# Hybrid encoder trunk on one core: the first feed-forward down projection multiplies 256 tokens at a time instead of 512

## The chip, the cores and the metric

The kernel runs on one core of one Trainium2 chip. The metric is the device time of one execution in microseconds (us), from the first to the last instruction of the program. The trace comes from one profiled execution on that core.

## The reference

Two layers, 512 frames (tokens) of 1024 features, everything in float32. Each layer does this:

```
x = x + 0.5 * swiglu(rmsnorm(x, ffn1_norm), ffn1_w_gate, ffn1_w_up, ffn1_w_down)
h = rmsnorm(x, mix_norm); proj = h @ w_in
x = x + concat(ssd_mixer(...), hgrn2_mixer(...)) @ w_out
x = x + 0.5 * swiglu(rmsnorm(x, ffn2_norm), ffn2_w_gate, ffn2_w_up, ffn2_w_down)

def swiglu(h, w_gate, w_up, w_down):
    return (jax.nn.silu(h @ w_gate) * (h @ w_up)) @ w_down
```

A last rmsnorm follows the second layer. The hidden width of a feed-forward part is 2816. The part of interest is the last product of swiglu in the first feed-forward part, `(512 x 2816) @ (2816 x 1024)`, once per layer.

## The kernel before, in words

Activations lie with features on the partitions and the 512 tokens along the free dimension, so x is 8 tiles of 128 x 512 and the hidden activations are 22 tiles of 128 x 512. Weights are cut into 128 x 128 pieces. A float32 product is made of three products of a reduced format (fp32r): each operand is split into a high part and a low part, and high·high, high·low and low·high are added up in one PSUM bank. `products` (L1463 to L1469) issues these three matmuls for one 128 x 128 weight piece against all 512 tokens: L1467 is weight high with activation high, L1468 weight high with activation low, L1469 weight low with activation high. The hardware loads the stationary weights anew for each of them, which the trace shows as one LDWEIGHTS (engine PEld) for each MATMUL (engine PE).

A feed-forward part has two stages. The up stage makes gate and up for 22 hidden tiles (44 weight blocks of 8 pieces), and VectorE and ScalarE turn them into the hidden tiles `ahi` and `alo`. The down stage (`down`, L1569 to L1580) makes the 8 output tiles in two calls of four: for each output tile it adds up 22 pieces, which come in three weight blocks of 8, 7 and 7 pieces (DN_PIECES), in one of two PSUM banks, 4 and 5 in turn. So a down stage has 8 x 22 = 176 weight pieces and 528 matmuls. There are four down stages, two to a layer; c is 0 in the first feed-forward part of a layer and 1 in the second.

The four engines and the DMA queue run each their own program, tied by semaphores. SyncE loads a weight block into one of four slots (`raw`), ScalarE makes its high part (`whi`, L536 in the down stage), GpSimd makes its low part (`wlo`, L481), TensorE multiplies, and its last matmul on a block frees the slot. When an output tile is complete, VectorE adds it to x (L985), ScalarE and VectorE split the new x into `hhi` and `hlo` for the next stage, which starts with the first of these tiles.

On TensorE the down stage is a hardware loop of two turns (`pe.Fori`) in layer 0's first part and in layer 1's second part; in the other two it is written out. One turn has 264 matmuls. The order on TensorE is that of the program text.

Of the kernel before, what the change touches and what calls it, by code (L numbers as in the profile page):

```python
# [13 lines left out]
P = 128  # L14
DEPTH = 2
T = 512
# [17 lines left out]
NS = 4  # L34
# [101 lines left out]
def trunk_kernel(nc, x_cols, cols, first_norm, logits, lead, up1, dn1, mix, dt_in, up2, dn2, out):  # L136
    ctx = ExitStack()
    with ctx:
        def sb(name, shape, dt=F32, at=ctx):
            return at.enter_context(nc.sbuf_tensor(name, shape, dt))  # L140
# [38 lines left out]
        whi = sb("whi", [P, NS, BW], F32R)  # L179
        wlo = sb("wlo", [P, NS, BW], F32R)  # L180
# [84 lines left out]
        def bank(i):  # L265
            return ps[:, i, :]
# [9 lines left out]
        DOWN, NORM = 4, 6  # L276
# [215 lines left out]
        def _(act):  # L492
# [37 lines left out]
            with act.Fori(0, DEPTH) as l:  # L530
# [163 lines left out]
                def keep_up(n):  # L694
                    for i, (nn, _, _) in enumerate(PBLOCKS):
                        if nn == n:
                            hi(MIX0 + i + NS)
# [758 lines left out]
        def _(pe):  # L1456
            mm = pe.matmul
# [5 lines left out]
            def products(dst, q, piece, moving, start, stop):  # L1463

                s = slice(piece * P, piece * P + P)
                mh, ml = moving
                mm(dst, whi[:, q, s], mh, start=start, stop=False)  # L1467
                mm(dst, whi[:, q, s], ml, start=False, stop=False)  # L1468
                return mm(dst, wlo[:, q, s], mh, start=False, stop=stop)  # L1469

            def norm_products(l, ph):
                pe.wait_ge(x_sum.sem, x_sum.upto(l, KD * ph - 1))
                for c in range(TC):
                    last = mm(bank(NORM)[:, c:c + 1], acc[:, c * P:(c + 1) * P], ones[:, 0:1],
                              start=True, stop=True)
                last.then_inc(norm_sum.sem, 1)

            def norm_turns(l, ph):
                pe.wait_ge(x_sum.sem, x_sum.upto(l, KD * ph - 1))
                for c in range(TC):  # L1480
                    last = pe.transpose(bank(NORM)[:, c * P:(c + 1) * P], acc[:, c * P:(c + 1) * P], ident[:])
                last.then_inc(norm_sum.sem, 1)
# [7 lines left out]
            def norm_spreads(l, ph):  # L1490
                pe.wait_ge(norm_rms.sem, norm_rms.upto(l, ph))
                spread(norm_spread, bank(NORM), rt)

            def h_tile(k):
                return hhi[:, k, :], hlo[:, k, :]

            for l in range(DEPTH):
                def ready(e, k=0):
                    pe.wait_ge(e.sem, e.upto(l, k))
# [11 lines left out]
                def ffn(c, wb):  # L1511
                    ph = 2 * c

                    def begin(i, q):
                        jj, kind = q // 2, q % 2
                        free = (g_out, u_out)[kind]
                        pe.wait_ge(free.sem, free.upto(l, NJ * c + jj - 2) + 2 * i)
                        pe.wait_ge(split.sem, split.upto(l, wb + q) + NS * i)

                    def begin_lead(q):  # L1520

                        jj, kind = q // 2, q % 2
                        free = (g_out, u_out)[kind]
                        pe.wait_ge(free.sem, free.upto(l, NJ * c + jj - 2))
                        pe.wait_ge(lead_split.sem, q + 1)
                        pe.wait_ge(split.sem, l * (W + q + 1) + 1)

                    def tile_products(q, k):
                        return products(bank(2 * (q % 2) + q // 2), q, k, h_tile(k), k == 0, k == KD - 1)

                    def up_staggered():


                        for step in range(KD + NS - 1):
                            for q in range(NS):
                                k = step - q
                                if k == 0:
                                    if c == 0:
                                        begin_lead(q)
                                    else:  # L1540
                                        begin(0, q)
                                        if q in (1, 2):
                                            ready(x_tile, KD + MIXED.index(3 - q))
                                if c == 0 and k == KD // 2:
                                    ready(split, wb + q)
                                if q == 0 and k < KD:
                                    ready(x_low, KD * ph - KD + k)
                                if 0 <= k < KD:
                                    last = tile_products(q, k)
                                if k == KD - 1:  # L1550
                                    last.then_inc(blk.sem, 1)
                            if step == KD - 2:
                                norm_turns(l, ph)
                            if step == KD:
                                norm_spreads(l, ph)

                    def up(i):
                        for q in range(NS):
                            begin(i, q)
                            for k in range(KD):  # L1560
                                last = tile_products(q, k)
                            last.then_inc(blk.sem, 1)

                    up_staggered()
                    written_out = 6 if c == 0 else 0
                    for i in range(1, 1 + written_out):
                        up(i)
                    with pe.Fori(1 + written_out, NJ // 2) as i:
                        up(i)  # L1569
                    def down(i):  # L1570
                        for mm4 in range(4):
                            pe.wait_ge(x_tile.sem, x_tile.upto(l, KD * ph + mm4 - 2) + 4 * i)
                            for s, (j0, j1) in enumerate(DN_PIECES):
                                w = wb + UP_BLOCKS + 3 * mm4 + s
                                ready(hid_low, NJ * c + j1 - 1)
                                pe.wait_ge(split.sem, split.upto(l, w) + 12 * i)
                                for j in range(j0, j1):
                                    last = products(bank(DOWN + mm4 % 2), w % NS, j - j0,
                                                    (ahi[:, j, :], alo[:, j, :]), j == 0, j == NJ - 1)
                                last.then_inc(blk.sem, 1)  # L1580

                    if (l, c) in ((0, 1), (1, 0)):
                        for i in range(2):
                            down(i)
                    else:
                        with pe.Fori(0, 2) as i:
                            down(i)
# [268 lines left out]
                for i, (n, k0, k1) in enumerate(PBLOCKS):  # L1856
                    w = MIX0 + i
# [12 lines left out]
                    for k in range(k0, k1):  # L1870
# [11 lines left out]
                        last = products(bank(n % 3), w % NS, k - k0, h_tile(k), k == 0, k == KD - 1)  # L1882
# [87 lines left out]
            for c in range(2):  # L1970
                turn(c, FRONT).then_inc(out_turned.sem, 1)
            turn(TC, BACK[:-1])
            norm_products(DEPTH, 0)
            turn(TC, BACK[-1:]).then_inc(out_turned.sem, 1)
            turn(TC + 1, BACK).then_inc(out_turned.sem, 1)
# [69 lines left out]
```

## Time and profile before

| | |
|---|---|
| time, median of 2 runs | 1926.78 us (1925.85 to 1927.71) |
| span of the profiled execution | 1927.2 us |
| TensorE busy (matmul) | 1919.3 us |
| TensorE busy (weight load) | 1579.1 us |
| VectorE, ScalarE, GpSimd busy | 754.3, 701.8, 904.0 us |
| matmuls in the trace | 10396 |
| of these in the four down stages | 2112 |

The profile gives no time of the profiled execution other than its span, 1927.2 us, which lies inside the spread of the two runs. A matmul's recorded duration includes its way through the array and overlaps the next matmul's, so durations of matmuls add up to more than the time they take. The pace of a stream of matmuls is read from the distance of their starts, or from the weight loads, of which one goes with each matmul: their busy time and the idle time before them together are the time that the stream took.

### The profile page before, as it was taken

The page shows a single profiled execution, that of the slowest core. Times are in us where ns is not written, and L with a number is a line of the kernel's source. Part 1 is how long each engine was busy: PE and PEld are TensorE (multiplying, and loading weights), DVE is VectorE, ACT ScalarE, POOL GpSimd, SP SyncE. Part 2 cuts the span into 40 slices and gives each one's busy share as a digit, 9 for nine tenths or more (in the row PEclk, how much of TensorE's full clock was granted, in tenths as well). Part 3 has the DMA queues.
Part 4 walks back from the last instruction along what each step waited for, and adds up shares of the span by engine and source line. Part 5 has one row for each costly group of instructions (what it writes and reads, how often), then busy time and mean ns, then how long its engine had stood idle before and what let it go on. Part 6 is the DMA issues. An engine that isn't in the chain of part 4 may idle for free.

```text
span 1927.2 us, 28344 instructions
## 1 busy us (share of the span) xinstructions
PE 1919.3 (100%) x10396; PEld 1579.1 (82%) x10396; DVE 754.3 (39%) x1209; ACT 701.8 (36%) x975; POOL 904.0 (47%) x550
## 2 busy tenths in 40 slices
PE   9999999999999999999999999999999999999999
PEld 7888888788788888888888888887878888888887
DVE  6222221389875322231132222214898752222312
ACT  5222222365643322222332222324556432222223
POOL 3444444466335544444444444444654444444443
PEclk9999999999999999999999999999999999999999
DMA  5332333322213333333323333332222223333332
GB/s 182 104 99 90 96 97 99 99 67 89 67 55 99 109 98 98 97 90 100 103 93 98 99 91 93 97 100 89 78 79 75 66 91 108 98 98 95 91 100 97
DMA packets 53504, 181.84 MB, mean 94 GB/s; under 512 B 6816, under 2 KB 6816, under 8 KB 53408
## 3 DMA queue, kind: packets, MB, share of 16 engines
q1 hardware_dynamic: 53264, 180.56, 30.1%
q8 instruction: 60, 0.98, 0.2%
q14 instruction: 36, 0.29, 0.1%
q10 hardware_dynamic: 144, 0.00, 0.0%
HBM read 178.45 MB, written 2.10 MB: 94 GB/s over the span
## 4 chain that ended last, share of the span: by engine, by line
PE 99%; DMA 0%; ACT 0%; DVE 0%; issue 0%; SPq 0%; ACTq 0%
PE ps L1467 31%; PE ps L1469 31%; PE ps L1468 31%; PE ps L1685 1%; PE ps L1602 1%; PE ps L1604 1%; PE ps L1603 1%; PE ps L1733 0%; PE ps L1799 0%; PE ps L1963 0%; PE ps L1746 0%; PE ps L1804 0%; DMA x<-in_x 0%; PE ps L1487 0%; PE ps L1783 0%; PE ps L1717 0%
## 5 line engine op out<-in xcount | busy, mean ns | idle before, releaser
L481 POOL TENSOR_TENSOR wlo<-raw,whi 128x1024 fp32r<-128x1024 f32 (+1 forms) x536 | 901.7, 1698 | 1015.2 <-ACT whi L542 553.6
L1467 PE MATMUL ps<-hhi,whi 128*128 128x512 f32 x1760 | 691.6, 393 | 2.2 <-DVE hlo L848 1.7
L1469 PE MATMUL ps<-hhi,wlo 128*128 128x512 f32 x1760 | 686.5, 390 | 0.0
L1468 PE MATMUL ps<-hlo,whi 128*128 128x512 f32 x1760 | 686.3, 390 | 0.0
L1467 PEld LDWEIGHTS ps<-hhi,whi 128*128 128x128 f32 x1760 | 330.9, 188 | 76.1 <-issue 4.1
L1469 PEld LDWEIGHTS ps<-hhi,wlo 128*128 128x128 f32 x1760 | 330.9, 188 | 69.6
L1468 PEld LDWEIGHTS ps<-hlo,whi 128*128 128x128 f32 x1760 | 331.0, 188 | 67.4
L1469 PE MATMUL ps<-ahi,wlo 128*128 128x512 f32 x704 | 274.1, 389 | 0.0
L1467 PE MATMUL ps<-ahi,whi 128*128 128x512 f32 x704 | 274.1, 389 | 0.0
L1468 PE MATMUL ps<-alo,whi 128*128 128x512 f32 x704 | 274.1, 389 | 0.0
L536 ACT ACTIVATE whi<-raw 128x1024 fp32r<-128x1024 f32 x168 | 177.2, 1055 | 265.3 <-PE ps L1469 246.0
L964 DVE TENSOR_TENSOR u<-ps,r 128x512 f32<-128x512 f32 x88 | 60.8, 691 | 368.5 <-PE ps L1469 368.5
L542 ACT ACTIVATE whi<-raw 128x1024 fp32r<-128x1024 f32 x176 | 183.5, 1045 | 38.9 <-PE ps L1469 38.9
L555 ACT ACTIVATE ahi<-u 128x512 f32 (+1 forms) x88 | 55.6, 632 | 389.1 <-DVE u L967 389.1
L985 DVE SCALAR_TENSOR_TENSOR x<-ps,x 128x512 f32<-128x512 f32 x32 | 22.1, 692 | 368.7 <-PE ps L1469 368.7
L1467 PEld LDWEIGHTS ps<-ahi,whi 128*128 128x128 f32 x704 | 132.2, 188 | 27.5
L1468 PEld LDWEIGHTS ps<-alo,whi 128*128 128x128 f32 x704 | 132.2, 188 | 27.4
L1469 PEld LDWEIGHTS ps<-ahi,wlo 128*128 128x128 f32 x704 | 132.2, 188 | 27.2
L551 ACT ACTIVATE g<-g 128x512 f32<-128x512 f32 x88 | 55.6, 631 | 237.9 <-DVE g L962 237.9
L962 DVE TENSOR_TENSOR g<-ps,r 128x512 f32<-128x512 f32 x88 | 60.8, 691 | 167.6 <-PE ps L1469 166.7
L969 DVE TENSOR_TENSOR alo<-u,ahi 128x512 f32 x88 | 66.1, 751 | 81.7 <-ACT ahi L555 81.7
L506 ACT ACTIVATE hhi<-x,par 128x512 fp32r<-128x512 f32 x48 | 34.6, 721 | 152.5 <-DVE x L985 132.8
(276 smaller groups left out, 1354.6 us busy)
## 6 DMA issues: line engine op xcount, KB each, us to landing
raw<-in_up SPq DMA_DIRECT2D x168, 512.0 KB, 3.4
raw<-in_mix SPq DMA_DIRECT2D x64, 512.0 KB, 3.4
raw<-in_dn SPq DMA_DIRECT2D x64, 448.0 KB, 3.3
raw<-in_dn SPq DMA_DIRECT2D x32, 512.0 KB, 3.5
raw<-in_lead SPq DMA_DIRECT2D x8, 512.0 KB, 3.5
x<-in_x SPq DMA_DIRECT2D x8, 256.0 KB, 6.2
raw<-in_lead SPq DMA_DIRECT2D x8, 256.0 KB, 6.3
raw<-in_mix SPq DMA_DIRECT2D x8, 256.0 KB, 2.5
```

Source lines behind the costliest of these rows:

```text
L481: low = pool.tensor_tensor(wlo[:, q, part], raw[:, q, part], whi[:, q, part].bitcast(F32), ALU.subtract)
L506: act.activation(hhi[:, m, :], x[:, m, :], ACT.Copy, scale=gain).then_inc(x_high.sem, 1)
L536: act.activation(whi[:, q, :], raw[:, q, :], ACT.Copy).then_inc(high.sem, 1)
L542: act.activation(whi[:, q, :], raw[:, q, :], ACT.Copy).then_inc(high.sem, 1)
L551: act.activation(g2[:, jj, :], g2[:, jj, :], ACT.Silu).then_inc(silu_g.sem, 1)
L555: act.activation(ahi[:, 2 * i + jj, :], u2[:, jj, :], ACT.Copy).then_inc(hid_high.sem, 1)
L962: made(g_out, tt(g2[:, jj, :], bank(jj), r[:], ALU.mult))
L964: made(u_out, tt(u2[:, jj, :], bank(2 + jj), r[:], ALU.mult))
L969: made(hid_low, tt(alo[:, 2 * i + jj, :], u2[:, jj, :], ahi[:, 2 * i + jj, :].bitcast(F32), ALU.subtract))
L1467: mm(dst, whi[:, q, s], mh, start=start, stop=False)
L1468: mm(dst, whi[:, q, s], ml, start=False, stop=False)
L1469: return mm(dst, wlo[:, q, s], mh, start=False, stop=stop)
```

## The change

In the down stage of the first feed-forward part (c is 0) of both layers, `half_products` takes the place of `products`. For one weight piece it issues the three matmuls on tokens 0 to 255, and then the same three on tokens 256 to 511. The first matmul of an output tile alone has the start flag; the second half's first matmul does not. Nothing else is different: the same weight pieces in the same order, the same waits at the same places, the same signal after the last matmul of a block. The down stage of the second feed-forward part keeps `products`.

```diff
+            def half_products(dst, q, piece, moving, start, stop):
+
+                s = slice(piece * P, piece * P + P)
+                mh, ml = moving
+                for t in range(2):
+                    cols = slice(t * T // 2, (t + 1) * T // 2)
+                    mm(dst[:, cols], whi[:, q, s], mh[:, cols], start=start and t == 0, stop=False,
+                       skip_group_check=True)
+                    mm(dst[:, cols], whi[:, q, s], ml[:, cols], start=False, stop=False, skip_group_check=True)
+                    last = mm(dst[:, cols], wlo[:, q, s], mh[:, cols], start=False, stop=stop, skip_group_check=True)
+                return last
+
@@ down(i)
                                 for j in range(j0, j1):
-                                    last = products(bank(DOWN + mm4 % 2), w % NS, j - j0,
+                                    multiply = products if c else half_products
+                                    last = multiply(bank(DOWN + mm4 % 2), w % NS, j - j0,
                                                     (ahi[:, j, :], alo[:, j, :]), j == 0, j == NJ - 1)
```

On TensorE, in the loop over layer 0's first down stage, between two weight blocks (the REGISTER_ALU rows prepare the waits for the next block), this stands in the kernel before:

```order
 L1468 MATMUL ps<-alo,whi 128x512
 L1469 MATMUL ps<-ahi,wlo 128x512
 L1572 REGISTER_ALU
 L1576 REGISTER_ALU
 L1467 MATMUL ps<-ahi,whi 128x512
 L1468 MATMUL ps<-alo,whi 128x512
 L1469 MATMUL ps<-ahi,wlo 128x512
```

and this in the changed one, at the same place:

```order
 L1479 MATMUL ps<-alo,whi 128x256
 L1480 MATMUL ps<-ahi,wlo 128x256
 L1584 REGISTER_ALU
 L1588 REGISTER_ALU
 L1477 MATMUL ps<-ahi,whi 128x256
 L1479 MATMUL ps<-alo,whi 128x256
 L1480 MATMUL ps<-ahi,wlo 128x256
 L1477 MATMUL ps<-ahi,whi 128x256
 L1479 MATMUL ps<-alo,whi 128x256
 L1480 MATMUL ps<-ahi,wlo 128x256
```

Three matmuls of 512 columns became six of 256, nothing stands between them, and the waits stayed at the block's edge.

## Rows read from the trace of the kernel before

**Rows 1.** The page, busy time of TensorE, and its granted clock in 40 slices.
```profile
span 1927.2 us, 28344 instructions
PE 1919.3 (100%) x10396; PEld 1579.1 (82%) x10396; DVE 754.3 (39%) x1209; ACT 701.8 (36%) x975; POOL 904.0 (47%) x550
...
PEclk9999999999999999999999999999999999999999
```

**Rows 2.** The page, the chain that ended last, share by engine.
```profile
PE 99%; DMA 0%; ACT 0%; DVE 0%; issue 0%; SPq 0%; ACTq 0%
```

**Rows 3.** Groups of instructions, the down stages: busy us, mean ns | idle before.
```profile
L1467 PE MATMUL ps<-ahi,whi 128*128 128x512 f32 x704 | 274.1, 389 | 0.0
...
L1469 PEld LDWEIGHTS ps<-ahi,wlo 128*128 128x128 f32 x704 | 132.2, 188 | 27.2
L1468 PEld LDWEIGHTS ps<-alo,whi 128*128 128x128 f32 x704 | 132.2, 188 | 27.4
L1467 PEld LDWEIGHTS ps<-ahi,whi 128*128 128x128 f32 x704 | 132.2, 188 | 27.5
```

**Rows 4.** Busy time by window: the two down stages that are changed.
```profile
core 0: us, PE busy (x) PEld busy (x) DVE busy (x) ACT busy (x) POOL busy (x), PEclk, DMA share, GB/s
250.20:369.90 119.70, 119.70 (x529) 99.15 (x529) 19.28 (x34) 33.93 (x39) 57.44 (x24) 1.00 0.33 99
...
1202.70:1322.40 119.70, 119.70 (x529) 99.10 (x529) 19.28 (x34) 33.92 (x39) 57.45 (x24) 1.00 0.33 99
```

**Rows 5.** Timeline, first down stage around the loop's turn: start us, us, instruction.
```profile
309.86 0.39 PE L1469 MATMUL ps<-ahi,wlo 128*128 128x512 f32 x1
309.86 0.19 PEld L1467 LDWEIGHTS ps<-ahi,whi 128*128 128x128 f32 x1
310.08 0.39 PE L1467 MATMUL ps<-ahi,whi 128*128 128x512 f32 x1
310.09 0.19 PEld L1468 LDWEIGHTS ps<-alo,whi 128*128 128x128 f32 x1
310.29 0.69 DVE L985 SCALAR_TENSOR_TENSOR x<-ps,x 128x512 f32<-128x512 f32 x1 [12.12 <-PE ps L1469]
310.31 0.39 PE L1468 MATMUL ps<-alo,whi 128*128 128x512 f32 x1
```

**Rows 6.** Timeline of PE in the first 12 us.
```profile
9.08 0.63 PE L1468 MATMUL ps<-hlo,whi 128*128 128x512 f32 x1
...
11.64 0.63 PE L1468 MATMUL ps<-hlo,whi 128*128 128x512 f32 x1
```

**Rows 7.** Timeline of PE after the last down stage.
```profile
1914.86 2.62 PE L1963 MATMUL ps<-g,x 128*128 128x128 f32 x22
1917.32 1.01 PE L1474 MATMUL ps<-ones,acc 128*128 128x1 f32 x8
1918.19 4.04 PE L1963 MATMUL ps<-g,x 128*128 128x128 f32 x34
```

**Rows 8.** Groups of weight loads by width: busy us, mean ns | idle before.
```profile
L1963 PEld LDWEIGHTS ps<-g,x 128*128 128x128 f32 x64 | 7.4, 192 | 0.1
...
L1474 PEld LDWEIGHTS ps<-ones,acc 128*128 128x128 f32 x8 | 1.0, 191 | 0.0
...
L1812 PEld LDWEIGHTS ps<-km,headsum 128*8 128x8 f32 x16 | 0.2, 87 | 1.1 <-ACT b L578 1.1
```

**Rows 9.** Waits in the first down stage (250 to 370 us): total us, times, longest.
```profile
DVE x L985 <- PE ps L1469: 81.3, 7, 12.4
POOL wlo L481 <- ACT whi L536: 57.7, 23, 4.2
ACT whi L536 <- PE ps L1469: 49.4, 16, 3.7
```

**Rows 10.** The page, the queue that brings instructions: packets, MB, share of 16 engines.
```profile
q8 instruction: 60, 0.98, 0.2%
```

## The prediction

> **What bounds the kernel now.** I read the page first. TensorE is busy 1919.3 of 1927.2 us at a granted clock of nine tenths or more in all 40 slices [rows 1], which is the 2.4 GHz level, and the chain that ended last is 99% TensorE [rows 2]. So whatever a matmul costs more or less comes out in the end almost undiminished, if it lies in a stage where nothing else is late. That is what the windows of the two changed stages are for: each lasts 119.7 us, TensorE works through all of it at clock 1.00, while VectorE has 19.28 us of work, ScalarE 33.93 and GpSimd 57.44 [rows 4]. The waits of the first of them say the same from the other side: VectorE waits for TensorE (81.3 us), ScalarE waits for TensorE (49.4), GpSimd for ScalarE (57.7), and TensorE is in no row as one who waits [rows 9]. Each of these engines has more than half of the stage to spare.
>
> The number that decides is therefore the pace of the matmuls, and the recorded 389 ns of one [rows 3] is not it, since neighbours overlap. The weight loads give it: 132.2 us busy and 27.5 idle for 704 of them, so 159.7/704 = 226.8 ns for one 512-column matmul; the timeline shows the same steps, 309.86, 310.08, 310.31 [rows 5].
>
> **What 226.8 ns consist of.** At 2.4 GHz 512 columns need 213.3 ns, so 13.5 ns are something else. In the kernel's first microseconds, with TensorE at its lower level, six steps take 11.64 − 9.08 = 2.56 us, 427 ns each [rows 6]; 512 columns at 1.2 GHz are 426.7 ns, and nothing is left over. So the 13.5 ns come from a part that keeps ahead of the slow clock and not of the fast one. The rows leave two readings: **a fixed cost for each matmul** (then a half costs it again), or **a slower pace of each column** (then a half costs half). The lower level hides both. No row has an fp32r matmul of fewer than 512 columns, so this price has to be bounded.
>
> **The second limit is the weight load.** Each half loads its 128 x 128 piece anew. A load is recorded at 188 ns [rows 3], which is longer than a 256-column matmul will stream. But the recorded length holds a fixed part: 8 columns of weights take 87 ns, 128 take 188 to 192 [rows 3, 8], so the columns themselves cost (188 − 87)/120 = 0.84 ns each, 108 ns for 128. The output transposes after the last stage show what a dense stream of such loads does: 22 matmuls of 128 columns from 1914.86 to 1917.32 us are 112 ns apart, though each has a load recorded at 192 ns; and eight matmuls with a single moving column take 1918.19 − 1917.32 = 0.87 us, 109 ns each [rows 7, 8]. The matmul has nothing to stream there, so 109 to 112 ns is the floor that a load sets, and loads overlap one another in their fixed part. In the down stage a load starts together with the matmul before it (310.08 and 310.09) [rows 5], so it runs under that matmul.
>
> **The change, part by part.**
> - Matmuls: two stages with 528 of 512 columns, 1056 in all, go; 2112 of 256 columns come, 1056 more. Every one has its load.
> - Price of a half. Streaming is 256/2.4 = 106.7 ns. Fixed reading: 106.7 + 13.5 = 120.2 ns, which is above the load's floor of 112, so the load stays hidden with 8 ns to spare. Column reading: 113.4 ns, just above the floor. Lower bound: the floor itself, 109 to 112. Upper bound: the load is not hidden at all and counts with its recorded 188 ns, or with 112 ns behind a full 106.7 ns of streaming, 219 ns. I take the fixed reading. A cost that shows at one pace and is gone at half of it fits both, but the plain matmuls of 128 columns at 112 ns have a few ns above their load's 108 too [rows 7], though only 128 columns long; this looks like a step from one instruction to the next rather than a tax on columns.
> - Per pair: 2 x 120.2 − 226.8 = +13.6 ns. Sum: 1056 x 13.6 ns = **+14.4 us**, 7.2 us in each stage.
> - The second half's three matmuls add to other columns than the first half's, and consecutive ones of a half add to the same 256 columns about 120 ns apart. The 128-column matmuls with plain float32 operands stand twice in the trace for each in the program (64 for 32 [rows 8]), so that two of them add to the same columns 112 ns apart without a longer step: no cost.
> - Instructions to fetch and issue: matmul and load 112 ns apart is already the pace of rows 7, so issue is no limit at 120. The loop's body doubles, from 264 to 528 matmuls. Before, the loop turns at about 310.08 us and its step is 0.23 us like any other [rows 5]. If the longer body were no longer held, a turn would wait for up to four packets of instructions; a packet takes 0.2% x 16 x 1927.2/60 = 1.0 us [rows 10]. There is one such turn in a changed loop (the other changed stage is written out), so 0 to 4 us. I put 0, and keep 4 for the range.
> - Waits: none is added or moved. Blocks come free later by 24 x 13.6 ns = 0.3 us at most, and ScalarE, GpSimd and the queue get that much longer for the next; VectorE's add still waits for TensorE. The next stage starts on TensorE as before. All of this costs nothing, since it hides under TensorE.
>
> The Trainium skill (Runtime: NRT & Kernel Launch, Instruction fetch mechanics) says that a taken branch whose target is outside a window of two 16 KiB pages stalls for a fetch. By it the longer body would stall, within the 0 to 4 us above; the trace's short body shows no stall.
>
> The profiled execution's span, 1927.2 us, is 0.4 above the median of the two runs; from the median the forecast is 1926.8 + 14.4 = **1941 us**, +0.7%.
>
> **The rivals.** 2% of the time, 38.5 us, is about what a measurement of this kernel can tell from no change; that is 36.5 ns per pair, or a half at 131.6 ns.
>
> 1. *The forecast*: half at 118 to 123 ns, 1937 to 1947 us with the fetches allowed for. Chance 0.50.
> 2. *The extra is a pace of columns*: half at 113.4 ns, pair at 226.8 ns, nothing changes: 1927 us; with a ns or two of friction against the load's floor up to 1932. For it: the exact disappearance at the lower clock. Against it: I know of no reason in the rows for a tax on columns. Chance 0.20.
> 3. *A step at the load's floor only*: 109 to 112 ns per half, pair 218 to 224 ns, −9 to −3 us, 1918 to 1924 us. It needs the 13.5 ns to be absent at 256 columns. Chance 0.06. The Trainium skill (TensorE: Matmul & The Clock Gate, Back-to-back issue gap) gives N/2.4 + 2.5 ns for isolated matmuls, an estimate of 109.2 ns for a half and 1918 us by the same sum; for 512 columns it would give 215.8, where this trace has 226.8, so it does not describe these matmuls.
> 4. *Load and stream are too near each other*: 112 against 107 ns leaves little, and a late load holds the next matmul a few ns each time: half at 124 to 131 ns, 1949 to 1964 us. Chance 0.12.
> 5. *The load comes into the open* (slower). The mechanism: an fp32r matmul may start only when its load has run its recorded 188 ns, a load may start only with the matmul before, and 256 columns no longer cover it. Place: every matmul of the two stages. A pair is then 376 ns, +149 ns x 1056 = +158 us, **2084 us**; with load and stream one behind the other (219 ns) 438 ns, +223 us, 2150 us. It decides from 131.6 ns per half on. For it: 188 ns stand in the rows of this stage, and no short fp32r matmul does. Against it: the plain loads of 192 ns at steps of 112, with the same cost per width. Chance 0.12, with a small part of rival 4 above the bound.
>
> That the change might not do what it says is excluded by the order of instructions; that it is faster by 2% would need halves below 95 ns, under what 256 columns need at 2.4 GHz: 0.01.
>
> **The numbers.** The likeliest case gives 1941 us. From 1921 to 1962 us the range holds cases 1 and 2 and nearly all of 4, and about half of 3, together 0.83. Faster by over 2% 0.01, within 2% 0.86, slower by over 2% 0.13.
>
> **What the profile afterwards would show.** The weight loads of the down stage's first part: busy and idle time over their count is the step; 120 ns confirms the fixed reading, 113 the column reading, 188 or more the open load. Each changed stage should last 126.9 us and the two unchanged ones 119.7 as before, with the granted clock at 1.00. A gap of some us in the middle of the first changed stage, and none in the second, would be the loop's turn. I am wrong if any engine but TensorE is waited for in these stages, or if the unchanged stages move.

## The result and the profile after

| | before | changed | ratio, 95% interval |
|---|---|---|---|
| first comparison, median us | 1926.78 (2 runs) | 1943.09 (2 runs) | 1.0085, 1.0056 to 1.0114 |
| repeated with more runs, median us | 1928.03 (7 runs) | 1942.90 (4 runs) | 1.0081, 1.0064 to 1.0098 |
| span of the profiled execution, us | 1927.2 | 1940.8 | |

The change costs 0.8% (12 to 19 us by the second interval). By the medians it is 16.3 us in the first comparison and 14.9 in the second. The forecast was 1941 us, +14.4 us. The loss lies inside the 2% that the prediction called no change, but it is clear of the noise.

The page of the changed kernel, in the lines that answer to [rows 1] and [rows 10]:

```profile
span 1940.8 us, 30456 instructions
...
PE 1932.5 (100%) x11452; PEld 1632.5 (84%) x11452; DVE 754.7 (39%) x1209; ACT 701.7 (36%) x975; POOL 904.0 (47%) x550
...
PEclk9999999999999999999999999999999999999999
...
q8 instruction: 66, 1.08, 0.2%
```

There are 1056 matmuls and as many loads more; the other engines' work is the same; TensorE stays at the upper level; six more packets of instructions come in.

The four down stages of the changed kernel, busy time by window (the first and third are changed, the others not); it answers to [rows 4]:

```profile
core 0: us, PE busy (x) PEld busy (x) DVE busy (x) ACT busy (x) POOL busy (x), PEclk, DMA share, GB/s
248.10:374.70 126.60, 126.60 (x1057) 126.60 (x1056) 19.30 (x34) 33.88 (x39) 57.48 (x24) 1.00 0.31 94
847.90:967.50 119.60, 119.60 (x529) 99.06 (x528) 22.07 (x33) 35.20 (x40) 57.60 (x24) 1.00 0.33 100
1208.20:1334.80 126.60, 126.60 (x1057) 126.60 (x1056) 19.30 (x34) 33.88 (x39) 57.46 (x24) 1.00 0.32 95
1808.80:1928.40 119.60, 119.60 (x529) 99.06 (x528) 22.07 (x33) 35.21 (x40) 57.59 (x24) 1.00 0.30 91
```

Each window holds a stage to within 0.1 us. The changed stages take 7.0 us more each, the unchanged ones what they took before. The column of PEld changed most: a load was under way 83% of the time (99.06 of 119.60), and is now all the time (126.60 of 126.60). That does not make the load the limit, since E3 below keeps PEld as busy and goes faster. The groups that gave the pace in [rows 3] are now these:

```profile
L1479 PE MATMUL ps<-alo,whi 128*128 128x256 f32 x704 | 199.2, 283 | 0.0
...
L1477 PEld LDWEIGHTS ps<-ahi,whi 128*128 128x128 f32 x704 | 135.2, 192 | 0.1
```

They no longer give it. Busy and idle time over the count is (135.2 + 0.1)/704 = 192 ns, the recorded length of a load and nothing else, because a load now begins before the one of the line before it has ended, and no idle time is left between them. The pace has to be read from the starts. The timeline of PE around 311 us of the changed kernel, half a stage in, at the loop's turn:

```profile
310.87 0.28 PE L1480 MATMUL ps<-ahi,wlo 128*128 128x256 f32 x1
310.99 0.28 PE L1477 MATMUL ps<-ahi,whi 128*128 128x256 f32 x1
311.11 0.28 PE L1479 MATMUL ps<-alo,whi 128*128 128x256 f32 x1
311.23 0.28 PE L1480 MATMUL ps<-ahi,wlo 128*128 128x256 f32 x1
311.35 0.28 PE L1477 MATMUL ps<-ahi,whi 128*128 128x256 f32 x1
```

From start to start it is 0.12 us, with no gap where the loop turns. A changed stage takes 126.71 us from its first matmul to the next stage's, which is 120.0 ns for each of 1056 matmuls, against 119.68 us and 226.7 ns for each of 528 before. Twice the difference of the stages, 7.03 us, is 14.1 us.

That accounts for the stages. The two profiled spans differ by 13.6 us, because two more things differ, with opposite signs. In the first microseconds, before any changed instruction, the changed kernel's profile is about 2 us ahead: its first down stage starts at 248.0 us, before at 250.2, where the profile of before had a stretch at the lower clock [rows 6]. This start differs from one execution to the next (247.2 us in E2, 250.8 in E4). And in layer 1's mixer TensorE stops once, where it did not stop before. The timeline of PE in the changed kernel:

```profile
1446.24 0.50 PE L1730 MATMUL ps<-vt,kdt 128*64 128x64 f32 x9
1447.83 0.33 PE L1730 MATMUL ps<-vt,kdt 128*64 128x64 f32 x3 [1.09 <-issue]
```

The wait is for nothing that another engine does ("issue"). The ninth of these matmuls starts at 1446.52 us and the tenth at 1447.83, 1.3 us later. E1's profile of the same kernel has the stop at the same matmul, 1.5 us long. A packet of instructions comes in on queue q8 from 1445.4 us on, so a wait for instructions is likely; the profile does not tie the packet to the matmul.

The stretch from the first to the second down stage of a layer, which holds the mixer, took 1.2 us longer in layer 1 and 0.6 us longer in layer 0; in E1's profile 1.4 and 0.0. So outside the start the traces give 14.1 + 1.8 = 15.9 us and 14.1 + 1.4 = 15.5 us, between the two timed differences of 14.9 and 16.3.

### The profile page after: what moved, and what is told of

Same layout as the page of the kernel before. It is cut to its first block, busy times and chain, and to the rows that moved or that the text cites. A ratio compares the mean times of both kernels' runs of the same rounds, so it can differ in the third digit from the quotient of the medians.

```text
span 1940.8 us, 30456 instructions
## 1 busy us (share of the span) xinstructions
PE 1932.5 (100%) x11452; PEld 1632.5 (84%) x11452; DVE 754.7 (39%) x1209; ACT 701.7 (36%) x975; POOL 904.0 (47%) x550
## 4 chain that ended last, share of the span: by engine, by line
PE 99%; DMA 0%; issue 0%; ACT 0%; DVE 0%; SPq 0%; ACTq 0%
PE ps L1467 26%; PE ps L1469 26%; PE ps L1468 26%; PE ps L1479 4%; PE ps L1480 4%; PE ps L1477 4%; PE ps L1698 1%; PE ps L1615 1%; PE ps L1617 1%; PE ps L1616 1%; PE ps L1746 0%; PE ps L1812 0%; PE ps L1976 0%; PE ps L1759 0%; PE ps L1817 0%; PE ps L1499 0%
## 5 line engine op out<-in xcount | busy, mean ns | idle before, releaser
L1479 PE MATMUL ps<-alo,whi 128*128 128x256 f32 x704 | 199.2, 283 | 0.0
L1480 PE MATMUL ps<-ahi,wlo 128*128 128x256 f32 x704 | 199.2, 283 | 0.0
L1477 PE MATMUL ps<-ahi,whi 128*128 128x256 f32 x704 | 199.2, 283 | 0.0
L1467 PE MATMUL ps<-ahi,whi 128*128 128x512 f32 x352 | 136.9, 389 | 0.0
L1468 PE MATMUL ps<-alo,whi 128*128 128x512 f32 x352 | 136.9, 389 | 0.0
L1469 PE MATMUL ps<-ahi,wlo 128*128 128x512 f32 x352 | 136.9, 389 | 0.0
L1477 PEld LDWEIGHTS ps<-ahi,whi 128*128 128x128 f32 x704 | 135.2, 192 | 0.1
L1479 PEld LDWEIGHTS ps<-alo,whi 128*128 128x128 f32 x704 | 135.2, 192 | 0.1
L1480 PEld LDWEIGHTS ps<-ahi,wlo 128*128 128x128 f32 x704 | 135.2, 192 | 0.0
```

The source lines that it names most:

```text
L1477: mm(dst[:, cols], whi[:, q, s], mh[:, cols], start=start and t == 0, stop=False, skip_group_check=True)
L1479: mm(dst[:, cols], whi[:, q, s], ml[:, cols], start=False, stop=False, skip_group_check=True)
L1480: last = mm(dst[:, cols], wlo[:, q, s], mh[:, cols], start=False, stop=stop, skip_group_check=True)
```

## Experiments

**E1. The changed kernel again, more runs.** No edit.

> The changed kernel itself, timed against the kernel before in more rounds. Fixed cost of 13.3 ns for each matmul: 1056 more matmuls, +14.1 us, ratio 1.0073. Pace of columns: no difference, ratio 1.000. The first two runs gave 1.0085 with an interval of 0.0057 in width, the trace +14.07 us in the two changed stages.

Ratio 1.0081, interval 1.0064 to 1.0098; stages of 126.7, 119.7, 126.7 and 119.7 us in its profile. The reading by pace of columns, with ratio 1.000 and stages of 119.7 us, is out.

**E2. Halves in all four down stages.**

```diff
-                                    multiply = products if c else half_products
+                                    multiply = half_products
```

> Halves in all four down stages, the suspected cost doubled. Fixed cost per matmul: 2112 more matmuls of 13.3 ns, +28.2 us, 1955 us, ratio 1.0146, each of the four stages 126.7 us. If the second feed-forward part hides some of it (its stage is followed by other work than the first's), less than 28 us. If a longer loop body costs a turn, its fourth stage is 1 to 4 us above 126.7.

1958.18 us, ratio 1.0157 (1.0140 to 1.0174), that is +30 us; layer 0's two down stages and layer 1's second by window:

```profile
247.20:373.90 126.70, 126.70 (x1057) 126.70 (x1056) 19.29 (x34) 33.88 (x39) 57.51 (x24) 1.00 0.31 94
847.00:973.60 126.60, 126.60 (x1057) 126.60 (x1056) 19.94 (x33) 35.16 (x40) 57.56 (x24) 1.00 0.32 95
1817.00:1943.60 126.60, 126.60 (x1057) 126.60 (x1056) 19.94 (x33) 35.16 (x40) 57.56 (x24) 1.00 0.29 86
```

Each of the four stages costs 7.0 us, 28.1 in all, hidden nowhere. The fourth stage is again one with a loop, and pays nothing for its turn. The other 2 us come from the mixers; the stretch with layer 1's is 3.2 us longer than before. TensorE stops there for 1.7 us, and soon after its granted clock is at the lower level for 3.4 us, with 512-column matmuls running; the timeline of PE and the window:

```profile
1453.74 0.45 PE L1698 MATMUL ps<-w 64*64 64x64 f32 x7 [1.49 <-issue]
```
```profile
1455.50:1458.90 3.40, 3.40 (x10) 2.62 (x9) 2.85 (x7) 0.30 (x1) 0.00 (x0) 0.50 0.43 146
```

**E3. Quarters in the first down stages.** The loop over t runs over four pieces of 128 tokens.

```diff
-                for t in range(2):
-                    cols = slice(t * T // 2, (t + 1) * T // 2)
+                for t, cols in enumerate([slice(t * P, t * P + P) for t in range(4)]):
```

> Four matmuls of 128 tokens for each product in the first down stages. If only the fixed cost counted, a quarter would take 53.3 + 13.3 = 66.7 ns and the four 266.7, so +40 ns for each of 1056 products, +42 us, about 1969 us. If the weight load sets a floor of 109 to 112 ns for fp32r as it does for the plain matmuls after the last stage, four take 436 to 448 ns, +209 to +221 ns, +221 to +234 us, about 2150 to 2160 us. If a load had to run its recorded 188 to 192 ns before its matmul, four take 752 to 768 ns, +555 to +571 us.

2281.82 us, one run, over 120 us above what the load's floor gave and far under what the recorded load would. The windows tell why (first stage before the loop's turn, first stage after it, third stage):

```profile
250.80:368.40 117.60, 117.60 (x1056) 117.60 (x1054) 11.07 (x22) 16.64 (x19) 28.48 (x12) 1.00 0.19 55
373.00:595.00 222.00, 222.00 (x1042) 222.00 (x1042) 6.13 (x9) 15.01 (x17) 27.05 (x12) 0.50 0.09 28
1432.90:1668.50 235.60, 235.60 (x2113) 235.60 (x2111) 19.24 (x34) 33.89 (x39) 56.95 (x24) 1.00 0.18 54
```

Where the clock is 1.00, a quarter takes 235.6/2112 = 111.6 ns: the load's floor holds for fp32r as it does for the plain matmuls of [rows 7], and the stage costs 235.8 − 119.7 = 116 us more, as expected. In the second half of the first stage the clock is 0.50 and a quarter takes 222.0/1042 = 213 ns. It begins with this, on the timeline of PE:

```profile
368.47 0.28 PE L1479 MATMUL ps<-ahi,wlo 128*128 128x128 f32 x1
370.95 0.32 PE L1476 MATMUL ps<-ahi,whi 128*128 128x128 f32 x1 [2.20 <-issue]
371.11 0.28 PE L1478 MATMUL ps<-alo,whi 128*128 128x128 f32 x1
...
372.12 0.42 PE L1478 MATMUL ps<-alo,whi 128*128 128x128 f32 x1
372.33 0.42 PE L1479 MATMUL ps<-ahi,wlo 128*128 128x128 f32 x1
```

After 1056 matmuls, at the loop's turn, TensorE gets no instruction for 2.5 us. About a microsecond after it resumes, the steps grow from 0.11 to 0.21 us and stay so, until the next stage's 512-column matmuls have run for 2 us. With the stop this half costs 108.8 us more than the same half at the upper level would; most of the other 12 us of the excess lie in the mixers.

That the stop is a wait for instructions shows in queue q8, which brings them (its packets are 60 before, 66 in the changed kernel and 89 here). From 370 to 595 us, when the loop's body runs for the second time, it brings ten packets:

```profile
q8 instruction: 10, 0.16, 0.3%
```

In the changed kernel's second turn (311.4 to 374.7 us) there is no packet on this queue, and none in the kernel before's (310 to 369.9 us).

**E10. E3 once more.**

> The kernel of e3 once more, for the granted clock. In e3 the first changed stage fell to the lower level in its second half and the second stage never did. If a matmul of 128 tokens every 112 ns is too little work for the upper level, the clock falls again in one or both stages, at a time that may differ, and the total lies between 2160 us (no fall) and well over 2280 us. If e3 was a single accident: 2160 us, both stages 235.8 us.

2277.06 us, one run, with the stop (2.3 us from start to start) at the same matmul and the same fall after it; the third stage again at 1.00:

```profile
370.00:591.90 221.90, 221.90 (x1042) 221.90 (x1042) 6.13 (x9) 15.01 (x17) 26.57 (x12) 0.50 0.09 28
1429.00:1664.60 235.60, 235.60 (x2113) 235.60 (x2111) 19.25 (x34) 33.90 (x39) 56.91 (x24) 1.00 0.18 54
```

**E11. E3 with the loop written out.**

```diff
-                    if (l, c) in ((0, 1), (1, 0)):
+                    if (l, c) in ((0, 0), (0, 1), (1, 0)):
```

> Quarters as in e3 and e10, but layer 0's first down stage is written out like layer 1's, with no loop. In e3 and e10 TensorE waited 2.5 and 2.3 us for instructions at the loop's turn (a body of 1056 matmuls), 3.6 us and 4.1 us after the wait began the granted clock was at its lower level, and it stayed there until matmuls of 512 columns came. If the wait is what set the clock off: no wait, no fall, both stages 235.8 us, total about 2160 us. If the short matmuls alone do it: the fall comes again in the first stage, total 2277 to 2282 us less the 2.5 us.

2169.74 us; the first stage by window, and the page's clock:

```profile
247.00:483.00 236.00, 236.00 (x2112) 235.84 (x2111) 19.26 (x34) 33.90 (x39) 57.24 (x25) 1.00 0.18 53
```
```profile
PEclk9999999999999999999999999999999999999999
```

The matmuls are the same and the stop is gone, and so is the fall: two runs with it fell and the one without it did not. The stop at the turn sets off the fall, and short matmuls alone do not. (The expectation's 4.1 us for E10 is a misreading: its steps grow from 368.0 us on, 3.0 us after the wait began at 364.97.)

The 10 us above the expected 2160 are not in the down stages (235.8 us each). In the profiles the stretches that hold the mixers are 3.2 us longer than before in layer 0 and 7.9 in layer 1, and the start is 2.5 us shorter. TensorE stops there for 1.7, 2.6 and 2.2 us from start to start, and after each of the last two the clock is at the lower level for 3.4 us; the first of these:

```profile
1619.70:1623.00 3.30, 3.30 (x18) 2.71 (x19) 3.23 (x11) 0.00 (x0) 0.00 (x0) 0.50 0.59 164
```

**E4. 320 and 192 tokens.**

```diff
-                for t in range(2):
-                    cols = slice(t * T // 2, (t + 1) * T // 2)
+                for t, cols in enumerate((slice(0, 320), slice(320, T))):
```

> Two matmuls for each product as in the change, but over 320 and 192 tokens. Fixed cost alone: 133.3 + 13.3 and 80 + 13.3 ns, 240.0 in all, the same as two halves, 1941 us, stages of 126.7 us. With a load floor of 109 to 112 ns for each matmul by itself: the 192-token ones take 109 to 112 ns, 255.7 to 258.7 ns in all, +29 to +32 ns for each of 1056 products, 1957 to 1961 us, stages of 135.0 to 136.6 us. If loads could run ahead by more than one matmul, the long ones would make up for the short ones and the pair would stay at 240.

1964.0 us, one run (its kernel before at 1928.0), stages of 136.1 us as the load's floor gave; the total is 3 us above its 1961, 1.4 of them a stop in layer 1's mixer. The timeline of PE, six matmuls of one product:

```profile
299.92 0.25 PE L1476 MATMUL ps<-ahi,whi 128*128 128x192 f32 x1
300.01 0.28 PE L1478 MATMUL ps<-alo,whi 128*128 128x192 f32 x1
300.12 0.28 PE L1479 MATMUL ps<-ahi,wlo 128*128 128x192 f32 x1
300.23 0.33 PE L1476 MATMUL ps<-ahi,whi 128*128 128x320 f32 x1
300.40 0.30 PE L1478 MATMUL ps<-alo,whi 128*128 128x320 f32 x1
300.54 0.31 PE L1479 MATMUL ps<-ahi,wlo 128*128 128x320 f32 x1
300.69 0.25 PE L1476 MATMUL ps<-ahi,whi 128*128 128x192 f32 x1
```

The six take 0.77 us. Over a stage it is 257.7 ns a pair, where halves take 240. Only this sum is measured. It is what the long one at 133.3 + 13.3 = 146.7 ns and the short one at the load's floor, 111 ns, make together, although the short one's columns and 13.3 ns would be 93.3. The starts move between the two kinds by up to 25 ns (0.09 before the second 192, 0.17 after the first 320), but the long matmuls do not make up for the short ones, as they would if loads ran ahead by more than one matmul.

**E6. Halves in another order.**

```diff
-                for t in range(2):
-                    cols = slice(t * T // 2, (t + 1) * T // 2)
+                for i, (weights, tile) in enumerate(((whi, mh), (whi, ml), (wlo, mh))):
+                    for t in range(2):
+                        cols = slice(t * T // 2, (t + 1) * T // 2)
+                        last = mm(dst[:, cols], weights[:, q, s], tile[:, cols], ...)
```

> Halves as in the change, in another order: both token halves with one pair of operands, then both with the next, so neighbours write different halves of the bank and the load of each second one is that of the first repeated. If only the number of matmuls and loads counts, the stages stay at 126.7 us and the time at 1941 to 1943 us. If adding to the same 256 columns 120 ns apart costs something, the stages get shorter, at most to 2112 steps of 113 ns (119.7 us each). If a repeated weight piece were not loaded again, shorter too.

1944.34 us, one run, stages of 126.7 us. Neighbours now write different halves and nothing is gained, so adding to the same columns 120 ns apart costs nothing. A piece that was just loaded is loaded again, at the same price.

**E5. Narrow loads, three lengths.** `wide` is 128 for the first piece of an output tile and 64 after it. The kernel leaves out half of the output features of the other pieces, so its output is not the reference's; it is there for the pace alone.

```diff
+                wide = P if start else HALF
+                s = slice(piece * P, piece * P + wide)
+                for t, cols in enumerate((slice(0, 256), slice(256, 384), slice(384, T))):
+                    to = dst[0:wide, cols]
```

> In the first down stages all pieces but the first of an output tile use 64 of the 128 output features (the other half of the sum is left out), so a weight load has 64 columns; the tokens are cut into 256, 128 and 128. Question: do the 13.3 ns belong to the matmul or to the load under it? Belongs to the matmul: 256 columns again every 120.0 ns, and 128 columns every 66.7 ns, since a load of 64 columns, 53 ns narrower than one of 128, has its floor at 56 to 59 ns. Belongs to the load's columns (128 of them cost 13.3, 64 cost 6.7): 113.3 and 60.0 ns. Load floor not dependent on its width: 128 columns stay at 112 ns.

1946.46 us, one run. Nine matmuls of one piece, from one 256 to the next, take 707 ns on average; three of the timeline's starts:

```profile
300.78 0.28 PE L1478 MATMUL ps<-ahi,whi 128*64 128x256 f32 x1
...
301.13 0.22 PE L1478 MATMUL ps<-ahi,whi 128*64 128x128 f32 x1
...
301.48 0.28 PE L1478 MATMUL ps<-ahi,whi 128*64 128x256 f32 x1
```

Over the stage three of 256 columns take 0.349 us, 116 ns each, and six of 128 take 0.358, 60 ns each. Neither is what a cost of 13.3 ns for every matmul gives (120.0 and 66.7). The columns alone are 640 ns, so 7.4 ns a matmul are left, close to the 6.7 of a load's share. The loop of this kernel's first down stage has 792 matmuls in its body, and turns without a stop.

**E9. Load width and length apart.** As E5 (most of each sum is again left out), in all four down stages, with 64 columns of weights in layer 0 and 32 in layer 1, one matmul of 512 in the first part and two of 256 in the second.

> All four down stages, pieces after the first of an output tile with narrow weights (the rest of the sum is left out): layer 0 loads 64 columns, layer 1 loads 32; the first feed-forward part streams 512 tokens in one matmul, the second streams two halves of 256. After e5 the extra time of a matmul looks like one that the load under it causes. If the load's columns set it (13.3 ns for 128): 64 columns cost 6.7 ns, 32 cost 3.3, whatever the stream: 220.0 and 113.3 ns in layer 0, 216.7 and 110.0 ns in layer 1. If it is a cost of each matmul: 226.7 and 120.0 ns in both layers. If it is a pace of columns that a narrower array relieves: the same share at 512 and at 256.

1935.58 us, one run. The windows, in the order 512 over 64, 256 over 64, 512 over 32, 256 over 32:

```profile
249.10:370.40 121.30, 121.30 (x529) 72.07 (x528) 19.28 (x34) 33.88 (x39) 57.66 (x24) 1.00 0.33 98
843.20:963.10 119.90, 119.90 (x1057) 119.90 (x1056) 22.08 (x33) 35.21 (x40) 57.73 (x24) 1.00 0.33 100
1203.80:1326.00 122.20, 122.20 (x529) 59.32 (x528) 19.29 (x34) 33.89 (x39) 57.70 (x24) 1.00 0.32 97
1799.30:1921.50 122.20, 122.20 (x1057) 114.40 (x1056) 19.93 (x33) 35.21 (x40) 57.56 (x24) 1.00 0.30 89
```

The narrow matmuls alone step by 229.9, 113.4, 231.7 and 115.6 ns; less their columns, 16.5, 6.7, 18.3 and 8.9 ns. No theory of the three holds: the extra is not a constant of the matmul, it does not shrink with the load (a narrower load makes the 512-column ones slower than the 226.7 of a full load), and it is not a share of the columns. Even the same matmul differs with its neighbours: 256 columns over 64 take 113.4 ns here, and 116 between the 128-column matmuls of E5. Where the 13.3 ns come from stays open.

**E7 and E8. The cross products in bfloat16**, tried as a way to be rid of the extra: E7 in the first down stages, E8 everywhere. The high·low and low·high matmuls read the upper halves of the same words:

```diff
+                s = slice(2 * piece * P + 1, 2 * piece * P + 2 * P, 2)
+                top = [t.bitcast(BF16)[:, 1::2] for t in (mh, ml)]
+                mm(dst, whi[:, q, piece * P:piece * P + P], mh, start=start, stop=False)
+                mm(dst, whi[:, q, :].bitcast(BF16)[:, s], top[1], start=False, stop=False)
+                return mm(dst, wlo[:, q, :].bitcast(BF16)[:, s], top[0], start=False, stop=stop)
```

> First down stages with 512 columns again; the two cross products (high with low, low with high) read the upper two bytes of the same tiles as bfloat16, at a step of four bytes, so that only one matmul in three is fp32r. If the 13.3 ns belong to fp32r: up to 13.3 ns less for each of 704 matmuls, -9.4 us against the kernel before, 1918 us, changed stages of 115.0 us; a change of format from one matmul to the next may take some of it. If they belong to every matmul with a load: no change, 1927 us. If reading every second two-byte element halves the pace: 704 x 213 ns, +150 us.

> The same in every use of the three products (5184 cross matmuls: 2592 pieces, two each). If the 13.3 ns belong to fp32r: up to -69 us against the kernel before, 1858 us, ratio 0.964; less where the up stage then waits for weights, since ScalarE and GpSimd get 6% less time for a block. If they belong to every matmul: 1927 us. If a step of two elements halves the pace: over +1000 us.

E7: 1935.58 us, ratio 1.0041 (1.0027 to 1.0055). E8: 1981.92 us, ratio 1.0286 (1.0268 to 1.0303). Both slower than before, and no expectation met. The timeline of E7, PE and PEld:

```profile
300.10 0.19 PEld L1477 LDWEIGHTS ps<-ahi,whi 128*128 128x128 f32 x1
300.12 0.60 PE L1477 MATMUL ps<-ahi,whi 128*128 128x512 f32 x1
300.55 0.10 PEld L1478 LDWEIGHTS ps<-alo,whi 128*128 128x128 bf16 x1 [0.27 <-issue]
300.56 0.40 PE L1478 MATMUL ps<-alo,whi 128*128 128x512 bf16 x1
300.57 0.10 PEld L1479 LDWEIGHTS ps<-ahi,wlo 128*128 128x128 bf16 x1
300.80 0.39 PE L1479 MATMUL ps<-ahi,wlo 128*128 128x512 bf16 x1
300.80 0.19 PEld L1477 LDWEIGHTS ps<-ahi,whi 128*128 128x128 f32 x1
```

The bfloat16 load after an fp32r matmul is recorded 0.43 us after that matmul's start, where every load so far started with it. But the fp32r matmul's own record starts 0.03 us after the bfloat16 matmul before it, and so holds the time in which that one still streamed. The starts around a change of format do not give a pace. From one bfloat16 matmul to the next it is 240 ns, more than the 227 of fp32r. The three of a piece take 701 ns instead of 680, so 21 ns x 2592 pieces = 54 us in E8, nearly all of the 54.8 that it lost. Format and step of four bytes were changed together, and no run tells which of them costs. Whether bfloat16 operands that lie side by side, grouped so that the format changes rarely, would gain was not tried.

## Why the prediction was right, point by point

- **TensorE alone sets the time**: right. Stages longer by 7.0 us each came out in the total, and E2's four as well. In the first changed stage VectorE's and ScalarE's waits for TensorE only grew (81.3 to 100.5 us and 49.4 to 54.2). The prediction's sign of being wrong, that any engine but TensorE is waited for, was put too widely: GpSimd waits for ScalarE, 57.7 us before [rows 9] and 64.4 now, at no cost. What had to be absent is a wait of TensorE, and it is.
- **The price of a half**: forecast 120.2 ns from 106.7 + 13.5, measured 120.0. The sum of 14.4 us is 14.1 us. The rival by column pace (1927 us) is excluded by E1 and E2, the one that saves (1918 to 1924) too.
- **The sign in the loads**: wrong. The prediction wanted the step from busy and idle time of the loads over their count, 120 ns for the fixed reading and 188 or more for the open load. Read so, the changed kernel gives 192 ns, and would have confirmed the wrong rival. The sum works only while idle time stands between the loads, as it did at 226.7 ns.
- **Why it should be so**: right only as far as it was used. With a full load of 128 columns the extra is 13.3 ns at 512 and at 256 columns (226.7, 120.0), and E4's pairs fit the same at 320, so it is a cost for each matmul and not for each column. But "a step from one instruction to the next" is no explanation: E5 and E9 show that it changes with the load's width in no simple way. The number came from one length, 512 columns, and that it carried over to 256 was argued, not known: this step held by luck as much as by reason, and the chance of 0.50 said so.
- **The load's floor of 109 to 112 ns, and its hiding under one matmul**: right, and decisive in how narrow it is. E3's quarters stand on it at 111.6 ns, and E4's 192-column matmuls by the sum of the pair; halves are above it by 8 ns. The slow rival, a load that counts with its recorded 188 ns, is excluded: the loads are recorded at 192 ns now and start every 120. Rival 4, friction between load and stream, did not show at 256 columns at all.
- **Instructions**: right for the place that was looked at, wrong in that it was the only one. The loop's turn costs nothing with a body of 528 matmuls, as put, nor with E5's 792; E3 shows that with 1056 it costs 2.5 us, and then much more by the clock. But TensorE then stops for 1.3 to 1.5 us in layer 1's mixer, a term that was put at 0. That the longer code moves what stands behind it, and so where packets end, is the likely cause and was not tested; the stop is there in E4 and E6 too (1.4 and 1.8 us), which have the same number of matmuls. The Trainium skill (Runtime: NRT & Kernel Launch, Instruction fetch mechanics) gives two sizes: a window of two pages for a branch, and elsewhere in the section 128 KiB for TensorE. The runs go against the first: loops of 528 and 792 matmuls with their loads turn without a wait. They are in keeping with the second, by which 1056 matmuls with their loads are an estimate of 2112 instructions against 2048 held, which does not fit, and E5's 792, 1584 instructions, do.
- **The sum**: 14.1 us in the stages and 1.4 to 1.8 in the mixers make 15.5 to 15.9; timed 14.9 and 16.3.

## What to carry to other kernels

Read a matmul's price as the larger of two numbers, its columns plus what the rows show beyond them (here 13.3 ns), and the floor of the load it hides (here 112 ns for 128 columns of float32 weights), from start to start and never from the recorded lengths. Cutting the moving side in two then costs one extra for each cut down to about 240 columns, an estimate from (111.6 − 13.3) x 2.4, and below that the load's floor takes over. When a change adds instructions, look for stops by "issue" everywhere behind it, in the densest code above all, and keep a loop's body short enough to turn without one (here 792 matmuls did and 1056 did not).

## What the runs showed of the hardware

- **One stop can halve the clock for a whole stage.** In E3 and E10 2.5 and 2.3 us without a matmul at the loop's turn were followed by the lower level for 225 and 229 us; E11, without the stop, had both stages at 1.00 with the same matmuls. At the lower level a matmul of 128 columns starts every 213 ns, twice its 107 ns of columns, and the level rose 2.1 and 4.8 us after 512-column matmuls began.
- **What comes after the stop sets what it costs.** With 512-column matmuls behind it the lower level lasted 3.4 us (E2, and twice in E11). The length of the stop alone does not tell whether the level falls: 1.7 us in E2's mixer was enough, while in E3's a stop of 2.5 us (1746.61 to 1749.11 us) left it at 1.00, and so did the changed kernel's 1.3 us.
- **A loop's body that is too long is brought in again at each turn.** With 1056 matmuls ten packets of instructions came in the second turn (E3), with 264, 528 and 792 none (before, changed, E5).
- **bfloat16 at a step of four bytes, in turn with fp32r, is slower than fp32r alone**: 701 ns for three matmuls of 512 columns against 680 (E7).
- **A narrower load can make a long matmul slower**: 226.7, 229.9 and 231.7 ns for 512 columns over 128, 64 and 32 columns of weights (E9).
